# A three-block transformer on one NeuronCore: two gate products before the recurrence half, one weight split put off, squares folded inside the output units

## The chip, the core and the metric

The kernel runs on one core of a Trainium2 chip. Five engines work side by side: TensorE (matmuls), VectorE, ScalarE, GpSimd (idle here) and SyncE, which issues the DMAs. They meet only at semaphores. The metric is the device time in microseconds of one execution.

## What is computed

The input is a sequence of 256 tokens with 1024 features, in fp32. Two blocks of a first kind are followed by one of a second kind. The change lies in the first kind, between its mixer and its feed-forward:

```
merged = sigmoid(ga) * (y_attn @ w_proj_attn[l]) + sigmoid(gb) * (y_hgrn @ w_proj_hgrn[l])
x = x + merged @ w_out[l]
h = rmsnorm(x, norm_ffn[l])
g, u = split(h @ w_ffn_in[l], 2)
x = x + (silu(g) * u) @ w_ffn_out[l]
```

`y_attn` comes from a sparse attention, `y_hgrn` from a chunked gated recurrence, both 512 wide. The block of the second kind (forgetting attention, a convolution of 31 taps, another feed-forward) is not touched.

## The kernel before

**Units.** All weights are read once, in units of at most 128 x 2048 values, in a fixed order (`plan_units`). Per block of the first kind there are projections, then 4 *merge* units (256 of the 1024 outputs each, an attention half with `w_proj_attn` and an hgrn half with `w_proj_hgrn`), 4 *output* units (`w_out`), and the feed-forward: gate 0, up 0, gate 1, up 1, down 0, gate 2 and so on. I number merges and outputs 0 to 3.

**Each weight is split in two.** A matmul of this kernel is done as three, high times high, high times low and low times high (`three`, lines 507 to 509). So every unit passes ScalarE, which rounds it to `w_hi` (line 928 through the helper `f`), and VectorE, which makes `w_lo = raw - w_hi` (line 1370, `split`). There are 6 slots for raw weights and 3 (`SPL`) for split ones. `split_ahead` splits the unit three ahead of the one in hand, so a high part can start when the unit three before it is done, and SyncE refills a raw slot when its `w_lo` is written. Activations are split in the same way (`h_hi`/`h_lo`, `ya`, `yh`, `x_gained`).

**The merges.** On TensorE `first_merges` runs the attention halves of merges 0 and 1, waits for the recurrence's `yh_lo`, and runs their hgrn halves; merges 2 and 3 follow whole. Each half goes to a PSUM bank of its own. On VectorE, in `mixer`, a merge unit is: product A (`mix_a` = attention bank times `gate_a`, line 1793), product B (`mix_b` = hgrn bank times `gate_b`, line 1795), their sum (line 1797), then, behind ScalarE's `h_hi`, the low part `h_lo` (line 1799), and a `split_ahead`. `mix_a` has two buffers, `mix_b` one.

**The outputs.** TensorE's output unit 0 takes its inputs pair by pair as the `h_lo` of merges 0 to 3 are marked (`g_lo`). On VectorE an output unit is: addition into `xT` (line 1806), low part of the gained pair (`x_gained_lo`, line 1423, behind ScalarE's `x_gained_hi`), and a `split_ahead`. ScalarE does the high part, the split, and the square of the pair into `h_norm`. Gate unit 0 takes the gained pairs in turn. After output 3 VectorE folds the squares of each pair into one (`squares_folded`, line 1401), and TensorE sums them over the partitions in `norm_sum` (line 629), between gate 0 and up 0.

The order on each engine is the order in which the code is written; nothing reorders it.

Of the kernel before, what the change touches and what calls it, by code (L numbers as in the profile page):

```python
# [21 lines left out]
ALU = mybir.AluOpType  # L22
# [25 lines left out]
SPL = 3  # L48
# [61 lines left out]
UOUT = {b: min(n for n, u in enumerate(UNITS) if u[:2] == ("out", b)) for b in range(3)}  # L110
# [75 lines left out]
def build(nc, a, out):  # L186
    base = (nc.sbuf_base + 31) // 32 * 32

    def at(name, shape, dt, off_kb):
        return nc.alloc_sbuf_tensor_at(name, shape, dt, offset=base + int(off_kb * 1024))[:]  # L190
# [43 lines left out]
    mixa = [at(f"mix_a{i}", [P, 512], F32, 163 + 2 * i) for i in range(2)]  # L234
# [3 lines left out]
    ga = at("gate_a", [P, KC, T], F32, 183)  # L238
# [108 lines left out]
    def lo_at(m):  # L347

        return split_lo, m + 1
# [35 lines left out]
            ("keys_set", 1), ("decayed", 16),  # L385
            ("pair_products", 18), ("recurrence_out", 2), ("o_squares", 2), ("o_sum", 2), ("o_rstd", 2),
            ("yh_set", 1), ("yh_hi_set", 1), ("yh_lo_set", 1), ("pairs_taken", 10), ("blocks_copied", 6)))
    r_diag = Event("diagonals_taken", 2)
    g_sig = Event("gates_set", 2)
    g_mix, g_hi, g_lo = Event("mixed", 4), Event("mixed_hi", 4), Event("mixed_lo", 4)  # L390

# [23 lines left out]
    def bank(m, i=0):  # L415
        return S[BANKS[m][0][i]]
# [85 lines left out]
    def _(pe):  # L502
        cur = [0]

        def three(dst, w_h, w_l, x_h, x_l, start, stop):

            pe.matmul(dst, w_h, x_h, start=start, stop=False, skip_group_check=True)  # L507
            pe.matmul(dst, w_h, x_l, start=False, stop=False, skip_group_check=True)  # L508
            return pe.matmul(dst, w_l, x_h, start=False, stop=stop, skip_group_check=True)  # L509

        def merge_half(m, half):

            hi = wh[m % SPL].rearrange("p (k n) -> p k n", k=KC)
            lo = wl[m % SPL].rearrange("p (k n) -> p k n", k=KC)
            x_h, x_l = (yh_h, yh_l) if half else (ya_h, ya_l)
            for n in range(2):
                for k in range(4):
                    ws = (slice(None), 4 * half + k, slice(P * n, P * n + P))
                    mm = three(bank(m, half)[:, T * n:T * n + T], hi[ws], lo[ws], x_h[:, k, :], x_l[:, k, :], k == 0, k == 3)
            return mm  # L520

        def first_merges(b):

            m = cur[0]
            cur[0] += 2
            pe.wait_ge(*a_lo.upto(b))
            for i in range(2):
                pe.wait_ge(*lo_at(m + i))
                for e, c in BANKS[m + i][1]:
                    pe.wait_ge(evac[e], c)  # L530
                merge_half(m + i, 0)
            pe.wait_ge(*r_lo.at(b))
            for i in range(2):
                merge_half(m + i, 1).then_inc(unit_done, 1)
# [383 lines left out]
    def _(act):  # L918
        lane = Lane("act_lane")
        cur = [0]  # L920
# [6 lines left out]
        def f(out_, in_, func, **kw):  # L927
            return act.activation(out_, in_, func, **kw)  # L928

        def split(m):  # L930
            if m >= len(UNITS):
                return
            act.wait_ge(landed[m % RAW], LANDED[m])
            if m >= SPL:
                act.wait_ge(unit_done, m - SPL + 1)
            n = held(m)
            f(wh[m % SPL][:, 0:n], raw[m % RAW][:, 0:n], ACT.Copy).then_inc(split_hi, 1)
# [4 lines left out]
        def split_ahead():  # L942

            split(cur[0] - 1 + SPL)

        def tick(n=1):

            for _ in range(n):
                step()
                split_ahead()  # L950
# [42 lines left out]
        def square(ni, j):  # L993
            f(hn[:, 2 * j:2 * j + 2, :], xT[:, 2 * j:2 * j + 2, :], ACT.Square).then_inc(*lane.mark(n_sq))
# [53 lines left out]
        def feed_forward(b):  # L1048
            if b < 2:
                f(ones_r, ones, ACT.Copy).then_inc(*lane.mark(ones_rounded))  # L1050
            if b == 2:
                rstd(rs, A[0][:, 0:T], D, n_ms.at(5), n_rs, load=False)
                normed_hi(5)
            for i in range(FS):
                tick()
                if shifted(UNITS[here()]):
                    shifted_in(sg[i].rearrange("p (c t) -> p c t", c=2), here(), ACT.Silu, g_silu)
                elif scaled_after(UNITS[here()]):
                    if i == 0:
                        rstd(rs, A[0][:, 0:T], D, n_ms.at(2 * b + 1), n_rs)  # L1060
                    act.wait_ge(*evacuated(here()))
                    f(sg[i % 2], sg[i % 2], ACT.Silu).then_inc(*lane.mark(sg_silu))
                    if i == 0:
                        normed_hi(2 * b + 1)
                else:
                    unit_in()
                    if i >= 2:
                        act.wait_ge(*f_gu.at(b, i - 2))
                    f(sg[i % 2], bank(here()), ACT.Silu).then_inc(*emptied())
                tick()  # L1070
                act.wait_ge(*f_gu.at(b, i))
                if i >= 2:
                    act.wait_ge(unit_done, UFF[b] + 3 * (i - 2) + 5)
                f(gu_h[i % 2].rearrange("p c t -> p (c t)"), gu, ACT.Copy).then_inc(f_hi.sem, 1)
                lane.last = f_hi.at(b, i)
                if b < 2 and i - 1 in ADA_STEPS:
                    for j in ADA_GROUPS[ADA_STEPS.index(i - 1)]:
                        n = ADA_LAYER * b + j + 1
                        act.wait_ge(ada_summed, n)
                        if n > 4:  # L1080
                            act.wait_ge(ada_done, n - 4)
                        f(ada_h[:, j % 4, :], ada_sum[:, j % 4, :], ACT.Copy).then_inc(ada_hi, 1)
                if i:
                    tick()
            step()
# [8 lines left out]
        def mixer(b, x_ready):  # L1094
# [158 lines left out]
            for j in range(4):  # L1253
                step()
                act.wait_ge(*evacuated(UOUT[b] + j))
                gained_hi(2 * b + 1, lambda k: pc("norm_ffn", 8 * b + k), j)
                split_ahead()
                square(2 * b + 1, j)
            feed_forward(b)

        def qk_rstd(b, i):
# [96 lines left out]
    def _(dve):  # L1358
        lane = Lane("dve_lane")
        cur = [0]  # L1360
        tt, ts_, stt = dve.tensor_tensor, dve.tensor_scalar, dve.scalar_tensor_tensor

        def split(m):
            if m >= len(UNITS):
                return
            dve.wait_ge(split_hi, m + 1)
            if m >= SPL:
                dve.wait_ge(unit_done, m - SPL + 1)
            n = held(m)
            tt(wl[m % SPL][:, 0:n], raw[m % RAW][:, 0:n], wh[m % SPL][:, 0:n].bitcast(F32), ALU.subtract)\  # L1370
                .then_inc(split_lo, 1)
            lane.last = lo_at(m)
# [1 line left out]
        def step():  # L1374
            cur[0] += 1

        def split_ahead():

            split(cur[0] - 1 + SPL)

        def tick(n=1):

# [4 lines left out]
        def here():  # L1387
            return cur[0] - 1
# [37 lines left out]
        def squares_folded(ni, pairs=range(4)):  # L1426
            for j in pairs:
                fold(j, n_sq.at(ni, j), n_fold)
# [251 lines left out]
        def mixer(b):  # L1680
# [71 lines left out]
            for g in range(2):  # L1752
                gs = slice(2 * g, 2 * g + 2)
# [30 lines left out]
            tt(yh_l, scr, yh_h.bitcast(F32), ALU.subtract).then_inc(*lane.mark(r_lo))  # L1784
            tick()
            dve.wait_ge(*g_sig.upto(b))
            for j in range(4):
                step()
                unit_in()
                gs = slice(2 * j, 2 * j + 2)  # L1790
                if j >= 2:
                    dve.wait_ge(*g_lo.at(b, j - 2))
                tt(mixa[j % 2], bank(here(), 0), ga[:, gs, :].rearrange("p c t -> p (c t)"), ALU.mult).then_inc(*lane.step())
                dve.wait_ge(*lane.last)
                tt(mixb, bank(here(), 1), gb[:, gs, :].rearrange("p c t -> p (c t)"), ALU.mult).then_inc(*emptied())
                dve.wait_ge(*lane.last)
                tt(mixa[j % 2], mixa[j % 2], mixb, ALU.add).then_inc(*lane.mark(g_mix))
                dve.wait_ge(*g_hi.at(b, j))
                tt(hl[:, gs, :].rearrange("p c t -> p (c t)"), mixa[j % 2],
                          hh[:, gs, :].rearrange("p c t -> p (c t)").bitcast(F32), ALU.subtract).then_inc(*lane.mark(g_lo))  # L1800
                split_ahead()
            for j in range(4):
                step()
                unit_in()
                x = xT[:, 2 * j:2 * j + 2, :].rearrange("p c t -> p (c t)")
                tt(x, bank(here()), x, ALU.add).then_inc(*emptied())
                gained_lo(2 * b + 1, lambda k: pc("norm_ffn", 8 * b + k), j)
                split_ahead()
            squares_folded(2 * b + 1)
            feed_forward(b)  # L1810
            if b:
                shift_lo(0)
# [129 lines left out]
        m = here()  # L1942
# [128 lines left out]
```

## Time and profile before

| | us |
|---|---|
| median of 3 runs | 1211.08 (1210.41 to 1212.88) |
| profiled execution, its own time | 1210.74 |
| its span, first to last instruction | 1209.0 |
| TensorE busy in the span | 1152.7 |
| VectorE / ScalarE busy | 862.9 / 622.2 |
| mean granted TensorE clock | 0.992 |

A timeline row has the start in us from the span's start, the duration in us, engine, line of the kernel, operation, output and inputs, shape and count. In brackets stands how long the engine had been idle before, and the instruction that released it. Consecutive matmuls overlap: the distance between two starts is what one costs. A row of the waiting list has the engine and line that waited, for whom, the total, how often, and the longest. A row of the windows has the stretch, its length, the busy time of TensorE with its count, the granted clock (1.00 is full speed), and the share and rate of the DMA engines. The stretch of interest is 200 to 252 us in block 0, and 621 to 674 us in block 1.

### The profile page before, as it was taken

The page shows a single profiled execution, that of the slowest core. Times are in us where ns is not written, and L with a number is a line of the kernel's source. Part 1 is how long each engine was busy: PE and PEld are TensorE (multiplying, and loading weights), DVE is VectorE, ACT ScalarE, POOL GpSimd, SP SyncE. Part 2 cuts the span into 40 slices and gives each one's busy share as a digit, 9 for nine tenths or more (in the row PEclk, how much of TensorE's full clock was granted, in tenths as well). Part 3 has the DMA queues.
Part 4 walks back from the last instruction along what each step waited for, and adds up shares of the span by engine and source line. Part 5 has one row for each costly group of instructions (what it writes and reads, how often), then busy time and mean ns, then how long its engine had stood idle before and what let it go on. Part 6 is the DMA issues. An engine that isn't in the chain of part 4 may idle for free.

```text
span 1209.0 us, 21217 instructions
## 1 busy us (share of the span) xinstructions
PE 1152.7 (95%) x8966; PEld 1115.6 (92%) x8966; DVE 862.9 (71%) x1404; ACT 622.2 (51%) x762; POOL 0.2 (0%) x4
## 2 busy tenths in 40 slices
PE   6999999999999999999999999999999989999996
PEld 5789899999999998998999999999988889999996
DVE  6996474777888779955757778887799757544543
ACT  7676336454434466753464544344587455443333
POOL 0000000000000000000000000000000000000000
PEclk9999999999999999999999999999999999999998
DMA  9555433656879555463336568795544332655511
GB/s 348 157 163 175 140 106 105 227 192 210 280 255 322 171 177 162 142 187 126 111 112 216 191 211 281 253 320 180 165 140 140 99 111 75 207 188 193 176 36 35
DMA packets 177615, 214.16 MB, mean 177 GB/s; under 512 B 3696, under 2 KB 160752, under 8 KB 177520
## 3 DMA queue, kind: packets, MB, share of 16 engines
q1 hardware_dynamic: 176800, 211.86, 53.4%
q8 instruction: 71, 1.16, 0.4%
q10 hardware_dynamic: 720, 0.94, 0.2%
q14 instruction: 24, 0.20, 0.0%
HBM read 211.74 MB, written 1.05 MB: 176 GB/s over the span
## 4 chain that ended last, share of the span: by engine, by line
PE 71%; DVE 19%; ACT 6%; issue 2%; DMA 1%; SPq 0%; DVEq 0%; ACTq 0%
PE stream L507 16%; PE stream L508 15%; PE stream L509 15%; DVE w_lo L1370 7%; PE steps L507 5%; PE steps L509 5%; PE steps L508 5%; PE steps L844 2%; ACT w_hi L928 2%; DVE conv_acc L1926 2%; PE steps L697 1%; PE stream L718 1%; DMA raw<-in_w_in 1%; ACT probs L928 1%; DVE h_norm L1450 1%
## 5 line engine op out<-in xcount | busy, mean ns | idle before, releaser
L1370 DVE TENSOR_TENSOR w_lo<-raw,w_hi 128x2048 fp32r<-128x2048 f32 (+2 forms) x178 | 401.4, 2266 | 205.3 <-ACT w_hi L928 203.7
L928 ACT ACTIVATE w_hi<-raw 128x2048 fp32r<-128x2048 f32 (+2 forms) x178 | 336.5, 1894 | 326.1 <-PE stream L509 294.2
L507 PE MATMUL stream<-h_hi,w_hi 128*128 128x256 f32 x1576 | 450.6, 286 | 12.1 <-DVE w_lo L1370 7.4
L509 PE MATMUL stream<-h_hi,w_lo 128*128 128x256 f32 x1576 | 446.5, 283 | 0.0
L508 PE MATMUL stream<-h_lo,w_hi 128*128 128x256 f32 x1576 | 446.5, 283 | 0.0
L507 PEld LDWEIGHTS stream<-h_hi,w_hi 128*128 128x128 f32 x1576 | 303.0, 192 | 16.3 <-DVE w_lo L1370 10.3
L508 PEld LDWEIGHTS stream<-h_lo,w_hi 128*128 128x128 f32 x1576 | 303.1, 192 | 0.5 <-issue 0.5
L509 PEld LDWEIGHTS stream<-h_hi,w_lo 128*128 128x128 f32 x1576 | 303.0, 192 | 0.0
L507 PE MATMUL steps<-gu_hi,w_hi 128*128 128x256 f32 x528 | 149.8, 284 | 1.4 <-DVE gu_lo L1665 1.4
L508 PE MATMUL steps<-gu_lo,w_hi 128*128 128x256 f32 x528 | 149.4, 283 | 0.0
L509 PE MATMUL steps<-gu_hi,w_lo 128*128 128x256 f32 x528 | 149.4, 283 | 0.0
L507 PEld LDWEIGHTS steps<-gu_hi,w_hi 128*128 128x128 f32 x528 | 101.3, 192 | 1.8 <-issue 1.8
L508 PEld LDWEIGHTS steps<-gu_lo,w_hi 128*128 128x128 f32 x528 | 101.3, 192 | 0.0
L509 PEld LDWEIGHTS steps<-gu_hi,w_lo 128*128 128x128 f32 x528 | 101.3, 192 | 0.0
L1619 DVE SCALAR_TENSOR_TENSOR ada_sum<-ada_raw,c_act,ada_sum 128x256 f32<-128x256 f32 x168 | 81.5, 485 | 6.0
L928 ACT ACTIVATE gu_hi<-gu 128x512 fp32r<-128x512 f32 x33 | 20.9, 633 | 102.6 <-DVE gu L1661 98.5
L580 PE MATMUL stream<-w_hi,x_gained_hi 128*128 128x512 f32 (+1 forms) x96 | 37.3, 388 | 11.3 <-DVE w_lo L1370 11.3
L1926 DVE SCALAR_TENSOR_TENSOR conv_acc<-conv_in,params,conv_acc 128x256 f32<-128x256 f32 x90 | 38.9, 488 | 1.0
L1665 DVE TENSOR_TENSOR gu_lo<-gu,gu_hi 128x512 fp32r<-128x512 f32 x33 | 22.9, 692 | 23.1 <-ACT gu_hi L928 23.1
L507 PE MATMUL stream<-x_gained_hi,w_hi 128*128 128x256 f32 x128 | 36.6, 286 | 0.0
L508 PE MATMUL stream<-x_gained_lo,w_hi 128*128 128x256 f32 x128 | 36.2, 283 | 0.0
L509 PE MATMUL stream<-x_gained_hi,w_lo 128*128 128x256 f32 x128 | 36.2, 283 | 0.0
(296 smaller groups left out, 1653.4 us busy)
## 6 DMA issues: line engine op xcount, KB each, us to landing
raw<-in_w_ffn_in SPq DMA_DIRECT2D x66, 1024.0 KB, 5.3
raw<-in_w_in SPq DMA_DIRECT2D x54, 1024.0 KB, 5.4
raw<-in_w_ffn_out SPq DMA_DIRECT2D x33, 1024.0 KB, 5.2
ada_raw<-in_ada_w SPq DMA_DIRECT2D x24, 1024.0 KB, 6.4
raw<-in_w_out SPq DMA_DIRECT2D x8, 1024.0 KB, 5.1
raw<-in_w_proj_attn SPq DMA_DIRECT2D x8, 512.0 KB, 3.5
raw<-in_w_proj_hgrn SPq DMA_DIRECT2D x8, 512.0 KB, 4.5
raw<-in_w_o SPq DMA_DIRECT2D x4, 1024.0 KB, 4.9
```

The costliest lines, as they stand in the source:

```text
L507: pe.matmul(dst, w_h, x_h, start=start, stop=False, skip_group_check=True)
L508: pe.matmul(dst, w_h, x_l, start=False, stop=False, skip_group_check=True)
L509: return pe.matmul(dst, w_l, x_h, start=False, stop=stop, skip_group_check=True)
L580: pe.matmul(dst, h_h[:, k0 + k, ts], hi[:, k, :], start=k0 + k == 0, stop=False)
L697: mm = pe.matmul(pv[:, DH * h:DH * h + DH], prT[:, h, s, :], v[:, s, DH * h:DH * h + DH], start=s == 0, stop=s == qt)
L718: mm = pe.matmul(conv_bank[:, 0:T], diag[j], upad[:, 3, j:j + T], start=j == 0, stop=j == CONV_K - 1)
L844: mm = pe.matmul(pair_bank(i, g)[:, c - 2 * g, t, :], hk[:, c, P * t:P * t + P], qp[:, c, P * tq:P * tq + P], start=True, stop=True)
L928: return act.activation(out_, in_, func, **kw)
L1370: tt(wl[m % SPL][:, 0:n], raw[m % RAW][:, 0:n], wh[m % SPL][:, 0:n].bitcast(F32), ALU.subtract)\
L1619: ins = stt(acc, w[:, k, :], cact[:, k:k + 1], acc, ALU.mult, ALU.add)
L1665: tt(gu_l[i % 2].rearrange("p c t -> p (c t)"), gu, gu_h[i % 2].rearrange("p c t -> p (c t)").bitcast(F32), ALU.subtract).then_inc(*lane.m ...
L1926: ins = stt(cv[:, c, :], src, w, cv[:, c, :], ALU.mult, ALU.add)
```

## The change

On TensorE the last matmul of the attention halves of merges 0 and 1 now steps a new semaphore, `merge_half`. On VectorE products A of merges 0 and 1 are issued together, when these halves are done and the gates are set, before the wait for merge 0; products A of merges 2 and 3 stay in their units. The `split_ahead` at the end of merge 2 (it makes the low part of output unit 1) is left out there and done behind the work of merge 3, ahead of that unit's own. In the output units the squares of pair j-1 are folded at the end of unit j, for j = 1 and 2, and those of pairs 2 and 3 in unit 3 ahead of its `split_ahead`, on both VectorE and (for the square) ScalarE.

```
@@ first_merges
-                merge_half(m + i, 0)
+                merge_half(m + i, 0).then_inc(m_half.sem, 1)
@@ ScalarE, output units
-                split_ahead()
+                if j < 3:
+                    split_ahead()
                 square(2 * b + 1, j)
+            split_ahead()
             feed_forward(b)
@@ VectorE, split_ahead
-        def split_ahead():
-
-            split(cur[0] - 1 + SPL)
+        def split_ahead(behind=(0,)):
+
+            for n in behind:
+                split(cur[0] - 1 + SPL - n)
@@ VectorE, merges
             dve.wait_ge(*g_sig.upto(b))
+
+            def gate_a(j):
+                tt(mixa[j % 2], bank(UOUT[b] - 4 + j, 0), ga[:, 2 * j:2 * j + 2, :].rearrange("p c t -> p (c t)"), ALU.mult)\
+                    .then_inc(*lane.step())
+
+            for j in range(2):
+                dve.wait_ge(*m_half.at(b, j))
+                gate_a(j)
             for j in range(4):
                 step()
                 unit_in()
                 gs = slice(2 * j, 2 * j + 2)
                 if j >= 2:
                     dve.wait_ge(*g_lo.at(b, j - 2))
-                tt(mixa[j % 2], bank(here(), 0), ga[:, gs, :].rearrange("p c t -> p (c t)"), ALU.mult).then_inc(*lane.step())
+                    gate_a(j)
...
-                split_ahead()
+                if j != 2:
+                    split_ahead(range(j // 3, -1, -1))
@@ VectorE, output units
                 gained_lo(2 * b + 1, lambda k: pc("norm_ffn", 8 * b + k), j)
-                split_ahead()
-            squares_folded(2 * b + 1)
+                if j < 3:
+                    split_ahead()
+                squares_folded(2 * b + 1, range(j - 1, j + j // 3) if j else ())
+            split_ahead()
             feed_forward(b)
```

On VectorE, at the start of the merges of block 0, stood before (`w_lo_60` is the low part of merge 2, `w_lo_58` that of merge 3; `mix_a_104` and `mix_a_105` are the two buffers):

```order
L1784 TENSOR_TENSOR yh_lo<-scratch,yh_hi 128x1024
L1370 TENSOR_TENSOR w_lo_60<-raw_51,w_hi_57 128x2048
L1793 TENSOR_TENSOR mix_a_104<-stream,gate_a 128x512
L1795 TENSOR_TENSOR mix_b<-stream,gate_b 128x512
L1797 TENSOR_TENSOR mix_a_104<-mix_a_104,mix_b 128x512
L1799 TENSOR_TENSOR h_lo<-mix_a_104,h_hi 128x512
L1370 TENSOR_TENSOR w_lo_58<-raw_52,w_hi_55 128x2048
L1793 TENSOR_TENSOR mix_a_105<-stream,gate_a 128x512
```

and stands now:

```order
L1787 TENSOR_TENSOR yh_lo<-scratch,yh_hi 128x1024
L1372 TENSOR_TENSOR w_lo_60<-raw_51,w_hi_57 128x2048
L1792 TENSOR_TENSOR mix_a_104<-stream,gate_a 128x512
L1792 TENSOR_TENSOR mix_a_105<-stream,gate_a 128x512
L1806 TENSOR_TENSOR mix_b<-stream,gate_b 128x512
L1808 TENSOR_TENSOR mix_a_104<-mix_a_104,mix_b 128x512
L1810 TENSOR_TENSOR h_lo<-mix_a_104,h_hi 128x512
L1372 TENSOR_TENSOR w_lo_58<-raw_52,w_hi_55 128x2048
```

Product A of merge 1 has moved from behind the split of merge 3 to directly behind product A of merge 0.

On VectorE, from the end of merge 2 through merge 3 to output unit 0 (`w_lo_60` is here the low part of output 1, `w_lo_58` that of output 2), stood before:

```order
L1799 TENSOR_TENSOR h_lo<-mix_a_104,h_hi 128x512
L1370 TENSOR_TENSOR w_lo_60<-raw_54,w_hi_57 128x2048
L1793 TENSOR_TENSOR mix_a_105<-stream,gate_a 128x512
L1795 TENSOR_TENSOR mix_b<-stream,gate_b 128x512
L1797 TENSOR_TENSOR mix_a_105<-mix_a_105,mix_b 128x512
L1799 TENSOR_TENSOR h_lo<-mix_a_105,h_hi 128x512
L1370 TENSOR_TENSOR w_lo_58<-raw_49,w_hi_55 128x2048
L1806 TENSOR_TENSOR xT<-stream,xT 128x512
```

and stands now:

```order
L1810 TENSOR_TENSOR h_lo<-mix_a_104,h_hi 128x512
L1792 TENSOR_TENSOR mix_a_105<-stream,gate_a 128x512
L1806 TENSOR_TENSOR mix_b<-stream,gate_b 128x512
L1808 TENSOR_TENSOR mix_a_105<-mix_a_105,mix_b 128x512
L1810 TENSOR_TENSOR h_lo<-mix_a_105,h_hi 128x512
L1372 TENSOR_TENSOR w_lo_60<-raw_54,w_hi_57 128x2048
L1372 TENSOR_TENSOR w_lo_58<-raw_49,w_hi_55 128x2048
L1818 TENSOR_TENSOR xT<-stream,xT 128x512
```

The low part of output 1 stands behind the fourth `h_lo` instead of ahead of the fourth product A.

On VectorE, from output unit 2 to the feed-forward (`w_lo_58` is the low part of up 0, `w_lo_59` that of gate 1, `w_lo_60` that of up 1), stood before:

```order
L1806 TENSOR_TENSOR xT<-stream,xT 128x512
L1423 SCALAR_TENSOR_TENSOR x_gained_lo<-xT,params,x_gained_hi 128x256 x2
L1370 TENSOR_TENSOR w_lo_58<-raw_52,w_hi_55 128x2048
L1806 TENSOR_TENSOR xT<-stream,xT 128x512
L1423 SCALAR_TENSOR_TENSOR x_gained_lo<-xT,params,x_gained_hi 128x256 x2
L1370 TENSOR_TENSOR w_lo_59<-raw_53,w_hi_56 128x2048
L1401 TENSOR_TENSOR h_norm<-h_norm 128x256 x4
L1370 TENSOR_TENSOR w_lo_60<-raw_54,w_hi_57 128x2048
```

and stands now:

```order
L1818 TENSOR_TENSOR xT<-stream,xT 128x512
L1426 SCALAR_TENSOR_TENSOR x_gained_lo<-xT,params,x_gained_hi 128x256 x2
L1372 TENSOR_TENSOR w_lo_58<-raw_52,w_hi_55 128x2048
L1404 TENSOR_TENSOR h_norm<-h_norm 128x256
L1818 TENSOR_TENSOR xT<-stream,xT 128x512
L1426 SCALAR_TENSOR_TENSOR x_gained_lo<-xT,params,x_gained_hi 128x256 x2
L1404 TENSOR_TENSOR h_norm<-h_norm 128x256 x2
L1372 TENSOR_TENSOR w_lo_59<-raw_53,w_hi_56 128x2048
L1372 TENSOR_TENSOR w_lo_60<-raw_54,w_hi_57 128x2048
```

Of the four folds (`h_norm<-h_norm`) one now stands ahead of the addition of output 3, one ahead of that of output 2, and two ahead of the split of gate 1.

## Rows read from the trace of the kernel before

**Rows 1.** The page, busy time, share of the span and instructions of each engine:

```profile
PE 1152.7 (95%) x8966; PEld 1115.6 (92%) x8966; DVE 862.9 (71%) x1404; ACT 622.2 (51%) x762; POOL 0.2 (0%) x4
```

**Rows 2.** What TensorE waited for, whole span: total, times, longest:

```profile
PE stream L507 <- DVE h_lo L1799: 3.8, 2, 1.9
```

**Rows 3.** Timeline of TensorE, block 0: attention half, merge 3 and output 0, sum of squares:

```profile
195.86 0.28 PE L507 MATMUL stream<-ya_hi,w_hi 128*128 128x256 f32 x1
...
218.77 0.28 PE L509 MATMUL stream<-yh_hi,w_lo 128*128 128x256 f32 x1
218.89 0.28 PE L507 MATMUL stream<-h_hi,w_hi 128*128 128x256 f32 x1
...
223.09 0.28 PE L509 MATMUL stream<-h_hi,w_lo 128*128 128x256 f32 x1
225.29 0.38 PE L507 MATMUL stream<-h_hi,w_hi 128*128 128x256 f32 x1 [1.92 <-DVE h_lo L1799]
...
250.54 1.99 PE L629 MATMUL steps<-h_norm,ones 128*128 128x256 f32 x8 [0.52 <-DVE h_norm L1401]
```

**Rows 4.** Timeline of TensorE, block 1, same places:

```profile
646.94 0.38 PE L507 MATMUL stream<-h_hi,w_hi 128*128 128x256 f32 x1 [1.92 <-DVE h_lo L1799]
...
673.60 1.99 PE L629 MATMUL steps<-h_norm,ones 128*128 128x256 f32 x8 [0.44 <-DVE h_norm L1401]
```

**Rows 5.** Windows of TensorE behind the two stops, clock in the fourth column:

```profile
226.00:229.00 3.00, 3.00 (x28) 1.00 0.90 281
...
648.10:651.50 3.40, 3.40 (x18) 0.50 1.02 336
651.50:655.00 3.50, 3.50 (x32) 1.00 0.69 267
```

**Rows 6.** Timeline of VectorE, block 0, merge 0 and the end of merge 3:

```profile
200.64 2.28 DVE L1370 TENSOR_TENSOR w_lo<-raw,w_hi 128x2048 fp32r<-128x2048 f32 x1
204.76 0.69 DVE L1793 TENSOR_TENSOR mix_a<-stream,gate_a 128x512 f32<-128x512 f32 x1 [1.84 <-PE stream L509]
205.49 0.69 DVE L1795 TENSOR_TENSOR mix_b<-stream,gate_b 128x512 f32<-128x512 f32 x1
...
208.21 2.29 DVE L1370 TENSOR_TENSOR w_lo<-raw,w_hi 128x2048 fp32r<-128x2048 f32 x1
...
224.55 0.69 DVE L1799 TENSOR_TENSOR h_lo<-mix_a,h_hi 128x512 fp32r<-128x512 f32 x1 [0.70 <-ACT h_hi L928]
225.16 2.29 DVE L1370 TENSOR_TENSOR w_lo<-raw,w_hi 128x2048 fp32r<-128x2048 f32 x1
```

**Rows 7.** Timeline of VectorE, block 0, output units 0 and 1 and the folds:

```profile
227.36 0.69 DVE L1806 TENSOR_TENSOR xT<-stream,xT 128x512 f32<-128x512 f32 x1
229.02 0.88 DVE L1423 SCALAR_TENSOR_TENSOR x_gained_lo<-xT,params,x_gained_hi 128x256 fp32r<-128x256 f32 x2 [0.98 <-ACT x_gained_hi L928]
...
233.04 0.68 DVE L1806 TENSOR_TENSOR xT<-stream,xT 128x512 f32<-128x512 f32 x1
...
250.07 1.42 DVE L1401 TENSOR_TENSOR h_norm<-h_norm 128x256 f32<-128x256 f32 x4
```

**Rows 8.** Timeline of ScalarE, block 0, gates, two weight parts, the last square:

```profile
200.78 1.92 ACT L928 ACTIVATE gate_b<-gate_b 128x2048 f32<-128x2048 f32 x1
204.75 1.92 ACT L928 ACTIVATE w_hi<-raw 128x2048 fp32r<-128x2048 f32 x1 [2.05 <-PE stream L509]
...
219.15 1.92 ACT L928 ACTIVATE w_hi<-raw 128x2048 fp32r<-128x2048 f32 x1 [0.29 <-PE stream L509]
...
247.73 0.61 ACT L928 ACTIVATE h_norm<-xT 128x512 f32<-128x512 f32 x1
```

**Rows 9.** Timeline of SyncE's DMA queue, block 0:

```profile
202.95 19.23 SPq L476 DMA_DIRECT2D raw<-in_w_ffn_in  x4
225.33 0.37 SPq L455 DMA_DIRECT2D ada_raw<-in_ada_w  x1
```

**Rows 10.** The page, DMA issues: count, KB of each, median us to landing:

```profile
raw<-in_w_ffn_in SPq DMA_DIRECT2D x66, 1024.0 KB, 5.3
```

More of the change, by code:

```diff
@@ L387, in build @@
             ("yh_set", 1), ("yh_hi_set", 1), ("yh_lo_set", 1), ("pairs_taken", 10), ("blocks_copied", 6)))
-    r_diag = Event("diagonals_taken", 2)
+    r_diag, m_half = Event("diagonals_taken", 2), Event("merge_half", 2)
     g_sig = Event("gates_set", 2)
```

## Prediction

> **What bounds the kernel now.** Read the busy times first: TensorE is busy for 1152.7 of 1209.0 us [rows 1], so only two things shorten this kernel: less idle time of TensorE, or a fuller clock. Next comes the view of what TensorE waits for. One of its rows is for `h_lo` of line 1799, 3.8 us in two pieces of 1.9 [rows 2], one in each of the two first blocks. Then the timeline shows the place. Output unit 0 starts at 218.89, takes its inputs pair by pair, and stops after 36 of its 48 matmuls, at 223.09; the next one starts at 225.29 [rows 3]. What it lacks is the low part of the fourth merged pair, which VectorE writes from 224.55 on [rows 6]. The normal distance between matmuls is 0.12 us (192 of them from 195.86 to 218.89 [rows 3]), so a unit of 48 takes 5.76 us and the stop costs 2.20 - 0.12 = 2.08 us. At the end of the same stretch the sum of squares (line 629) waits another 0.52 us for the folded squares, and starts at 250.54 [rows 3]. The second block has the same rows 421.65 us later, with a stop that ends at 646.94 and the sum of squares at 673.60 [rows 4].
>
> From stop to sum of squares block 0 takes 250.54 - 225.29 = 25.25 us, block 1 takes 673.60 - 646.94 = 26.66. The windows explain the difference: behind the first stop the granted clock stays 1.00, while behind the second it is 0.50 from 648.1 to 651.5 (1.2 instead of 2.4 GHz) and then 1.00 again [rows 5]. So this profiled run paid 26.66 - 25.25 = 1.41 us for a dip that came 1.2 us after TensorE had stood still for 2.08.
>
> VectorE is what TensorE waits for here. Per merge unit it does product A, product B, their sum, the low part (behind ScalarE's high part), and one weight low part `w_lo`. From A to the start of the next `w_lo` it is 208.21 - 204.76 = 3.45 us, and `w_lo` takes its place for 227.36 - 225.16 = 2.20 [rows 6, 7]: 5.65 us in all. Merges 0 to 3 keep it busy without a gap from 204.76 to 227.36, while TensorE, which does the hgrn halves of merges 0 and 1 in 2.88 us each, is through with merge 3 at 218.89.
>
> **The change, part by part, in block 0.** I follow VectorE through the new order, always with the old rows' distances.
>
> *Products A of merges 0 and 1 early.* They need the attention halves (done by 201.61, 48 matmuls after 195.86), and still wait for the gates: `gate_b` is ready at 200.78 + 1.92 = 202.70 [rows 8], the `w_lo` ahead ends at 200.64 + 2.28 = 202.92 [rows 6]. Two products of 0.69 then end by 204.3, in the 1.84 us in which VectorE was idle until 204.76 [rows 6]. They cost nothing; without that cover they would cost up to 1.4. Product B of merge 0 now starts at 204.76. That saves 0.73 (204.76 to 205.49 [rows 6]), but ScalarE is on `w_hi` until 204.75 + 1.92 = 206.67 [rows 8], and the high part comes behind it, so only 0.37 is left: the next `w_lo` starts at 207.84 instead of 208.21. Merge 1 is 5.65 - 0.73 = 4.92 us: 212.76. Merge 2: product A at 212.76 + 2.20 = 214.96, end of its work at 218.41.
>
> *Low part of output unit 1 put off.* VectorE would now be free at 218.41, but merge 3 is released only at 219.15 (ScalarE's `w_hi`, held by the same unit, starts then [rows 8]). So product A starts at 219.15, and the low part of pair 3 ends 3.45 + 0.08 later (225.24 against 225.16 [rows 6]), at 222.68. TensorE wants it at 223.09 + 0.12 = 223.21. The stop of 2.08 us is gone, with 0.5 us to spare. What is late next is the weight part that was put off: `w_lo` of output 1 runs from 222.60 to 224.88, and TensorE wants it at 218.89 + 5.76 = 224.65. I take a new stop of 0.3 us there (bounds 0.2 to 0.6), output 1 starting at 224.95. `w_lo` of output 2 follows to 227.08, and has until 230.7.
>
> *Its DMA.* The slot that this low part frees was refilled at the end of SyncE's row, 202.95 + 19.23 = 222.18 [rows 9]; it becomes 224.9. Queued behind it are one modulation load, which waited until 225.33 anyway [rows 9], and one down-projection load. The refilled slot is read at 249 at the earliest, so 24 us cover a transfer whose median to landing is 5.3 us [rows 10]. I put it at nothing.
>
> *Squares folded inside the output units.* An addition into `xT` starts at 227.00, 0.36 earlier than the 227.36 of before. A VectorE round there was 233.04 - 227.36 = 5.68 us [rows 7], 0.08 under TensorE's. One fold is 1.42 / 4 = 0.36 [rows 7]. Rounds 1 and 2 carry one each, so the fourth addition starts at 227.00 + 17.04 + 0.72 = 244.76, and the low part of its gained pair ends 1.66 + 0.88 later [rows 7], at 247.30. TensorE reaches gate unit 0 at 224.95 + 0.1 for the restart + 17.28 = 242.33 and wants that pair 4.32 later, at 246.65. So part of the gain is given back: a second new stop of 0.7 us. The folds are the price (0.72), and their return is that the sum of squares no longer waits: folds 2 and 3 end near 248.0, before the last 12 matmuls of gate 0 do. These run from 247.35, and the sum of squares starts at 247.35 + 0.1 + 1.44 + 0.16 = 249.05. Against 250.54 that is **1.49 us**.
>
> ScalarE's square of pair 3 ahead of the last `w_hi` is what lets fold 3 go at 247.6; behind it, it was over only at 247.73 + 0.61 = 248.34 [rows 8]. The `w_hi` goes back by 0.6, and its `w_lo` ends near 251.0 with the next unit due at 256.6. From there on TensorE waits for nothing until the end of the feed-forward, so the lead of 1.49 carries through.
>
> The new semaphore step at the end of each attention half: the last matmul of merge 3, which has such a step, is at 218.77 and the next at 218.89, the usual 0.12 [rows 3], so four more cost nothing. The Trainium skill (TensorE: Matmul & The Clock Gate, section The cost: per-tile semaphore tail) counts about 26 ns for each increment; by that, as an estimate, four would be 0.1 us and the forecast 1206.8. The trace does not agree.
>
> **Sum.** Block 0: 1.49. Block 1, same rows 421.65 later: sum of squares at 646.94 + (249.05 - 225.29) = 670.70 instead of 673.60, so 2.90, of which 1.41 is the clock, if TensorE, with 0.3 and 0.7 us stops in place of 2.08, keeps it. Together 4.39: 1210.74 (this execution; its span is 1209.0) becomes 1206.35. The median of before is 1211.08, 0.34 above the profiled run: **1206.7 us**.
>
> **Rivals.**
>
> *The clock dip is luck.* Two equal stops were followed by one dip, so a run may have none, one or two, and the median of before need not hold the one I count; or it comes again after the new stops. Then only 2 x 1.49 = 2.98 is left: 1208.1. For it: block 0 kept its clock after the same stop. Against it: the dip that there is follows a stop. The Trainium skill (TensorE: Matmul & The Clock Gate, section The HAM clock gate) takes idle TensorE as the cause of a halved clock and says that its moment varies between runs of one kernel; the two blocks agree with the second half of that.
>
> *The stop only moves.* In merge 3 the high part must not be behind `w_hi` of output 2, which ends at 219.15 + 1.92 = 221.07 against the 221.33 at which it is wanted: 0.26 to spare. If this or the put-off `w_lo` comes a microsecond later than in my walk, output 1 waits 1.3 instead of 0.3, VectorE is late by as much in the output rounds, and a block gains about 0.5: 1210.1 without the clock, within the noise.
>
> *The folds hold VectorE up (slower).* Fold j-1 waits for ScalarE's square, which stands behind a `w_hi` of 1.9 us. If each of the two folds ahead of additions 2 and 3 waited that long, gate unit 0 would stop 3.8 us longer per block: 1206.7 + 7.6 = 1214.3. It turns slower than before from a wait of 1.1 us per fold (4 x 1.1 = 4.4). Against it: each fold stands a round of 5.7 us behind the square of its pair, and ScalarE is through with the last square at 248.34, 1.7 us before the first fold starts now [rows 7, 8], so it is not the late one there.
>
> **How the numbers follow.** Forecast 0.52, the dip as luck 0.27, the moved stop 0.14, the folds 0.05, 0.02 for what I don't see. For the range I take the forecast with its bounds (0.2 to 0.6 at output 1, a restart of 0.1 more or less at each stop, 0.7 us between medians of three): from 1205.6. Up it takes in the second case with the same spread: 1209.0. What can be told from no change is about 0.2%, 2.4 us, thus 1208.66: all of the forecast and most of the second case lie below, 0.79 with the rest; the moved stop and the tail of the second make 0.16; the folds 0.05.
>
> **What would show it.** In the changed trace: two products A back to back before 204.7; no wait for `h_lo` of pair 3; instead one of some 0.3 us for `w_lo` at output 1 and one of some 0.7 for `x_gained_lo` at gate unit 0; the sum of squares at 249.05 (670.7 in block 1) with no wait of its own; a granted clock of 1.00 in both stretches. I am wrong if the `h_lo` wait is still there, if either new wait is above 1.5 us, or if the clock is 0.50 somewhere between 205 and 260 or 627 and 680.

## The result, and the profile after

| | before | after |
|---|---|---|
| median, us | 1211.51 (4 runs, 1210.41 to 1212.88) | 1204.97 (4 runs, 1204.12 to 1205.77) |
| ratio, 95% interval | | 0.9949 (0.9937 to 0.9961) |
| profiled execution, its own time | 1210.74 | 1204.12 |
| its span | 1209.0 | 1202.3 |
| mean granted clock in it | 0.992 | 0.996 |

The changed kernel is 6.5 us faster, 4.4 had been forecast (the median of before was 1211.08 then), and the range, whose lower end was 1205.6, does not hold 1204.97.

The page's busy times come first. TensorE's is 3.8 us smaller than in [rows 1], with the same number of matmuls: matmuls at half clock last longer, so a part of the gain looks like clock; the windows further down show where.

```profile
PE 1148.9 (96%) x8966; PEld 1112.0 (92%) x8966; DVE 862.7 (72%) x1404; ACT 621.2 (52%) x762; POOL 0.2 (0%) x4
```

The timeline of TensorE in block 0, the places of [rows 3]. This execution stands 0.18 us later than the old one at 196.04 (195.86 there), so distances from that row are to be compared:

```profile
196.04 0.28 PE L507 MATMUL stream<-ya_hi,w_hi 128*128 128x256 f32 x1
...
224.72 0.28 PE L509 MATMUL stream<-h_hi,w_lo 128*128 128x256 f32 x1
225.07 0.39 PE L507 MATMUL stream<-h_hi,w_hi 128*128 128x256 f32 x1
...
246.65 0.28 PE L509 MATMUL stream<-x_gained_hi,w_lo 128*128 128x256 f32 x1
247.42 0.39 PE L507 MATMUL stream<-x_gained_hi,w_hi 128*128 128x256 f32 x1 [0.49 <-DVE x_gained_lo L1426]
...
248.84 0.28 PE L509 MATMUL stream<-x_gained_hi,w_lo 128*128 128x256 f32 x1
248.95 0.81 PE L629 MATMUL steps<-h_norm,ones 128*128 128x256 f32 x3
```

Output 0 runs through: the wait for `h_lo` is gone. Output 1 starts 0.35 behind its predecessor's last matmul instead of 0.12, a stop of 0.23 (0.3 forecast). Gate unit 0 stops for 0.77 - 0.12 = 0.65 us before its fourth pair (0.7 forecast), and the sum of squares follows the last matmul of gate 0 by 0.11 without a wait. Block 1 shows the same. From here on I use one measure, **D**: the distance from the first matmul of merge 0's attention half to the first matmul of the sum of squares. Before it is 250.54 - 195.86 = 54.68 us in block 0 [rows 3], and after it is 248.95 - 196.04 = 52.91; 52.92 in block 1.

VectorE in the same stretch, to set against [rows 6] and [rows 7]:

```profile
200.82 2.29 DVE L1372 TENSOR_TENSOR w_lo<-raw,w_hi 128x2048 fp32r<-128x2048 f32 x1
203.02 1.28 DVE L1792 TENSOR_TENSOR mix_a<-stream,gate_a 128x512 f32<-128x512 f32 x2
204.88 0.69 DVE L1806 TENSOR_TENSOR mix_b<-stream,gate_b 128x512 f32<-128x512 f32 x1 [0.57 <-PE stream L509]
...
207.40 0.69 DVE L1810 TENSOR_TENSOR h_lo<-mix_a,h_hi 128x512 fp32r<-128x512 f32 x1 [1.11 <-ACT h_hi L928]
...
219.28 0.69 DVE L1792 TENSOR_TENSOR mix_a<-stream,gate_a 128x512 f32<-128x512 f32 x1 [0.42 <-PE stream L509]
...
222.12 0.69 DVE L1810 TENSOR_TENSOR h_lo<-mix_a,h_hi 128x512 fp32r<-128x512 f32 x1 [0.70 <-ACT h_hi L928]
222.73 4.49 DVE L1372 TENSOR_TENSOR w_lo<-raw,w_hi 128x2048 fp32r<-128x2048 f32 x2
227.13 0.68 DVE L1818 TENSOR_TENSOR xT<-stream,xT 128x512 f32<-128x512 f32 x1
...
244.82 0.68 DVE L1818 TENSOR_TENSOR xT<-stream,xT 128x512 f32<-128x512 f32 x1
246.48 0.88 DVE L1426 SCALAR_TENSOR_TENSOR x_gained_lo<-xT,params,x_gained_hi 128x256 fp32r<-128x256 f32 x2 [0.98 <-ACT x_gained_hi L928]
247.28 0.75 DVE L1404 TENSOR_TENSOR h_norm<-h_norm 128x256 f32<-128x256 f32 x2
```

The two products A are over at 204.3, under TensorE's hgrn half of merge 0. In merge 3 VectorE now waits for TensorE (0.42), where in the old kernel TensorE waited for VectorE's low part. The two weight parts that follow merge 3 stand one behind the other, and the fourth addition starts at 244.82 - 0.18 = 244.64 on the old clock, against 244.76 in the prediction's walk.

The windows show the full clock where the old kernel had 1.00 in one block and 0.50 in the other [rows 5]:

```profile
226.00:229.00 3.00, 3.00 (x27) 1.00 0.98 303
...
646.00:650.00 4.00, 4.00 (x36) 1.00 1.06 361
```

The clock differs in a third place, which the change does not touch. In the third block TensorE stands still for 5.6 us, and the clock goes to one half towards the end of it. These are windows of the kernel before, then of the changed one:

```profile
996.30:999.70 3.40, 2.20 (x10) 0.50 0.00 0
999.70:1003.00 3.30, 3.30 (x14) 0.50 0.00 0
...
991.70:995.00 3.30, 2.79 (x13) 0.50 0.00 0
995.10:998.40 3.30, 3.30 (x23) 1.00 0.00 0
```

Set against each other matmul by matmul, the two profiled executions part at these places:

| where | us gained |
|---|---|
| block 0, merges to the first low-part matmul of up 0 (252.49 - 195.86 = 56.63 before, 250.80 - 196.04 = 54.76 after) | 1.87 |
| one matmul of the recurrence in block 1 | 0.40 |
| block 1, the same stretch as in block 0 | 3.29 |
| third block, half clock for 3.4 us instead of 6.8 | 1.28 |
| start of the kernel | -0.18 |

These make the 6.6 us between 1210.74 and 1204.12.

### The profile page after: what moved, and what is told of

Read it like the earlier page. It is cut to its first block, busy times and chain, and to the rows that moved or that the text cites. A ratio compares the mean times of both kernels' runs of the same rounds, so it can differ in the third digit from the quotient of the medians.

```text
span 1202.3 us, 21221 instructions
## 1 busy us (share of the span) xinstructions
PE 1148.9 (96%) x8966; PEld 1112.0 (92%) x8966; DVE 862.7 (72%) x1404; ACT 621.2 (52%) x762; POOL 0.2 (0%) x4
## 3 DMA queue, kind: packets, MB, share of 16 engines
q8 instruction: 71, 1.16, 0.4%
## 4 chain that ended last, share of the span: by engine, by line
PE 71%; DVE 18%; ACT 7%; issue 2%; DMA 1%; SPq 0%; DVEq 0%; ACTq 0%
PE stream L507 16%; PE stream L509 15%; PE stream L508 15%; DVE w_lo L1372 7%; PE steps L507 5%; PE steps L509 5%; PE steps L508 5%; ACT w_hi L928 3%; PE steps L844 2%; DVE conv_acc L1940 2%; PE steps L697 1%; PE stream L718 1%; DMA raw<-in_w_in 1%; ACT probs L928 1%; DVE h_norm L1453 1%
```

## Experiments

The kernels of one group ran on the same chip beside runs of the kernel before. Each diff is against the changed kernel.

### One part taken back at a time

**e1, products A back in their units.**

```
-            for j in range(2):
-                dve.wait_ge(*m_half.at(b, j))
-                gate_a(j)
             for j in range(4):
...
-                    gate_a(j)
+                gate_a(j)
```

> The changed kernel, with the products A of merges 0 and 1 back in their units. D is the distance from the first matmul of the attention half of merge 0 to the first matmul of the sum of squares; it is 54.68 us before and 52.91 after in block 0. By the walk of the prediction product A costs VectorE 0.73 once more, of which 0.37 was hidden by ScalarE's high part, so all that follows is 0.36 later: no stop for h_lo (0.15 us spare), a stop of 0.6 at output 1, one of 0.65 at gate unit 0, D = 53.3 in both blocks, 0.7 us slower in all than the changed kernel. Rival, the early products carry the gain: the stop for h_lo comes back with over 1 us, D = 54 or more.

Measured: D = 53.32 in both blocks, stops of 0.63 at output 1 and 0.66 at gate unit 0, none for `h_lo`; 1205.98 us, ratio to before 0.9955 (0.9938 to 0.9971). In D the early products are worth 0.4 us a block, not more. Two waits of VectorE hide the rest of what they save: the one for `h_hi` in merge 0 (1.11 instead of 0.70 in e1) and the one for TensorE in merge 3 (0.42). They also take away the 0.40 of the recurrence in block 1, as told below.

**e2, low part of output 1 back in merge 2.**

```
-                if j != 2:
-                    split_ahead(range(j // 3, -1, -1))
+                split_ahead()
```

> The changed kernel, with the low part of output unit 1 back in merge 2. By the walk the fourth h_lo is ready at 224.1 (before's clockwork), so output 0 stops for 0.9 us, output 1 and gate unit 0 not at all, and the sum of squares starts at the same place within 0.2 us: D = 53.0, time as the changed kernel's within 0.4 us. Rival, the put-off part is what removes the stop and is worth it: D is 0.9 or more longer (53.8), 1.8 us slower in all.

Measured: D = 53.08, 1205.47 us, ratio 0.9952 (0.9937 to 0.9966). The wait for `h_lo` is back, shorter than before:

```profile
224.56 0.39 PE L507 MATMUL stream<-h_hi,w_hi 128*128 128x256 f32 x1 [0.99 <-DVE h_lo L1810]
```

It is 1.16 us (I had 0.9), and it costs only 0.17 in D, because with it go the two stops of the changed kernel, 0.23 at output 1 and 0.65 at gate unit 0: VectorE's first addition starts 30.57 us behind merge 0 instead of 31.09, TensorE arrives later, and it waits neither at gate unit 0 nor at the sum of squares.

**e3, folds and last square back at the end.**

```
-                if j < 3:
-                    split_ahead()
-                squares_folded(2 * b + 1, range(j - 1, j + j // 3) if j else ())
-            split_ahead()
+                split_ahead()
+            squares_folded(2 * b + 1)
```

(and on ScalarE the last `split_ahead` ahead of the last `square`)

> The changed kernel, with the four folds back behind the last split of the output units and ScalarE's last square behind its last weight part. By the walk gate unit 0 doesn't stop, but VectorE reaches the folds only at 249.7, so the sum of squares waits some 2 us: D = 54.3, 1.4 us more per block than the changed kernel, 2.8 in all. Rival, the removed stop is the gain whatever the folds do: D = 52.3 (the changed kernel less its stop of 0.65 at gate unit 0).

Measured: D = 54.26 and 54.27; 1209.62 us (10 runs), ratio 0.9987 (0.9977 to 0.9996). The wait for `h_lo` is gone here too, and nearly all of its time has come up again at the sum of squares:

```profile
249.88 0.72 PE L629 MATMUL steps<-h_norm,ones 128*128 128x256 f32 x1 [1.87 <-DVE h_norm L1402]
```

That is a stop of 2.03 us, and in both blocks the clock fell right behind it (windows of TensorE in e3):

```profile
250.00:253.40 3.40, 3.40 (x9) 0.50 0.83 258
673.20:676.60 3.40, 3.40 (x13) 0.51 0.91 296
```

### One part alone

**e4, folds alone** (the edits of e1 and e2 together).

> Only the folds are moved: products A and the low part of output 1 stand as before. By the walk the stop of 2.08 us for h_lo stays, gate unit 0 doesn't stop, the sum of squares doesn't wait: D = 54.0, 0.7 us less per block than before. If the dip of the clock follows the stop of 2.08 us, a dip shows in at least one of the two blocks here as in the kernel before, and the time is 1.4 us or more above what D says (1211.5 - 1.4 = 1210.1 with before's dips). Rival, dips fall anywhere: the clock rows of e1, e2 and e3, which have no such stop, show as many between 205 and 260 or 625 and 680.

Measured: D = 54.00 in block 0 and 55.50 in block 1, where the clock fell 1.0 us after the end of the stop of 2.07; 1209.14 us (10 runs), ratio 0.9986 (0.9976 to 0.9995). The forecast time of 1210.1 was 1 us too high; 0.7 of that is its base, 1211.5, where the kernel before had a median of 1210.76 beside e4. Traces of kernels without a stop of 2 us (e1, e2) show no dip in these stretches.

**e9, early products alone** (the edits of e2 and e3 together).

> Only the products A of merges 0 and 1 are moved. The stop for h_lo shrinks to that of e2 (1.16 us), and the additions into xT run 1.1 us ahead of before until they meet TensorE's end of output 3, after which the folds stand behind the last split as before: D = 53.8, 0.9 us less per block than before, and no dip of the clock. Rival, the sum of squares is held by the folds wherever the stop is: D = 54.3 or more.

Measured: D = 53.74 and 53.75, a stop of 1.15 for `h_lo` and one of 0.66 at the sum, no dip in either block; 1207.03 us, ratio 0.9961 (0.9946 to 0.9976).

**e10, put-off part alone** (the edits of e1 and e3 together).

> Only the low part of output 1 is put off. No stop for h_lo, one of 0.63 us at output 1 as in e1; VectorE's additions start where they did before, and the folds stand at the end: D = 54.6, as before's 54.7 although the stop of 2.08 is gone; the sum of squares waits for the folds by over 1.5 us instead, and if that wait reaches 2 us a dip can follow it as in e3. Rival, the removed stop shows in the time: D = 53.2.

Measured: D = 54.67 in both blocks, within 0.01 that of the kernel before without a dip; 1210.83 us (10 runs), ratio 0.9997 (0.9987 to 1.0006). The stop of 2.08 is replaced by these two:

```profile
225.78 0.39 PE L507 MATMUL stream<-h_hi,w_hi 128*128 128x256 f32 x1 [0.48 <-DVE w_lo L1370]
...
251.02 0.48 PE L629 MATMUL steps<-h_norm,ones 128*128 128x256 f32 x1 [1.85 <-DVE h_norm L1402]
```

In block 1 a dip followed the second of these stops, and none did in block 0.

Alone, the early products, the put-off part and the folds save 0.94, 0.01 and 0.68 us of D, 1.63 together; with each other 1.77. None of them alone brings the 2.08 us of the list of waits: with the folds last, the sum of squares waits for them, and with the folds moved alone the stop stays. Two of them can even be worse than one: early products with the put-off part (e3) have D = 54.26, early products alone (e9) 53.74. In e3 VectorE waits 0.42 for TensorE in merge 3 with the put-off weight part still ahead of it, so the first addition starts 31.09 us behind merge 0 instead of 30.57, and the folds at the end are later by these 0.52.

### The stop that the change brought in

**e5, all folds in output unit 3.** The new stop at gate unit 0 is the price of the two folds ahead of additions 2 and 3. Behind the fourth `x_gained_lo` there is room for all four.

```
-                squares_folded(2 * b + 1, range(j - 1, j + j // 3) if j else ())
+                squares_folded(2 * b + 1, range(4 if j == 3 else 0))
```

> The changed kernel, with all four folds in output unit 3, between its x_gained_lo and its split, instead of one each at the end of units 1 and 2. By the walk the fourth x_gained_lo comes 0.72 us earlier, which ends the stop of 0.65 at gate unit 0, and the four folds (1.42 us) still end 0.1 us before the last matmul of gate 0. D goes from 52.91 to 52.2 in both blocks, the time from the changed kernel's by -1.4 us. Rival, the stop moves to the sum of squares, which waits for the folds: D stays at 52.7 or more.

**e6, the changed kernel again**, beside it.

> The changed kernel once more, as the measure for e5 and for the clock. D = 52.9 in both blocks, no dip of the clock between 190 and 260 or 610 and 680, median 1205.0.

Measured: e5 D = 52.25 and 52.24, 1203.67 us (5 runs, 1202.49 to 1204.69), ratio to before 0.9938 (0.9925 to 0.9950); e6 D = 52.93 and 52.92, 1204.63 us (5 runs, 1203.98 to 1205.28), ratio 0.9947 (0.9934 to 0.9959). D is 0.68 less per block, as expected; the medians differ by 1.0 us, where 1.4 was expected, within the spread of the runs. VectorE and TensorE in e5:

```profile
245.40 0.88 DVE L1426 SCALAR_TENSOR_TENSOR x_gained_lo<-xT,params,x_gained_hi 128x256 fp32r<-128x256 f32 x2 [0.98 <-ACT x_gained_hi L928]
246.20 1.43 DVE L1404 TENSOR_TENSOR h_norm<-h_norm 128x256 f32<-128x256 f32 x4
247.73 2.29 DVE L1372 TENSOR_TENSOR w_lo<-raw,w_hi 128x2048 fp32r<-128x2048 f32 x1
```

```profile
247.75 0.28 PE L509 MATMUL stream<-x_gained_hi,w_lo 128*128 128x256 f32 x1
247.86 0.60 PE L629 MATMUL steps<-h_norm,ones 128*128 128x256 f32 x2
```

The folds end at 247.63 and the sum starts at 247.86, with no bracket. By D and by the median this is the fastest kernel of the study; the intervals of its ratio and of e6's overlap.

**e11, e5 with the low part of output 1 back in merge 2.**

> As e5 (products A early, folds in output unit 3), with the low part of output 1 back in merge 2. TensorE stops 1.16 us for h_lo as in e2 and nowhere else: D = 53.1, 0.85 more than e5, so that the put-off part is worth five times what it is in e2 against the changed kernel (0.16). Rival, its worth is the same 0.16 with any place of the folds: D = 52.4.

Measured: D = 53.09 in both blocks; 1204.75 us, ratio 0.9943 (0.9928 to 0.9958). So the put-off part is worth 0.84 us a block once VectorE is not the bound at gate unit 0, 0.17 in the change as it was made, and nothing by itself (e10).

### The clock

**e7, e8 and e12, the kernel before again**, for more traces of its two stops.

> The kernel before once more. D = 54.7 in a block without a dip, 56.1 in one with. If each stop of 2.08 us is followed by a dip with a chance well over one half, the mean granted clock over all its runs is 0.003 below the changed kernel's (two dips of 3.4 us at half clock are 3.4 us of lost clock). If dips fall anywhere, the two kernels have the same mean clock.

> The kernel before for a third trace: two more stops of 2.08 us, to count how many are followed by a dip. Dips from the stops: at least one of the two. Dips anywhere: none, since the other kernels' traces show none in these stretches without a stop of 2 us.

> The kernel before for a fourth trace, to count dips behind its two stops of 2.08 us: with four dips behind six stops so far, one or two are expected; none would bring it to four of eight.

Measured: e7 1211.12 us (11 runs; ratio 1.0001, 0.9992 to 1.0010), D = 56.09 and 56.08, a dip behind both stops; e8 D = 54.66 and 56.09 in 1210.49 us; e12 54.67 and 56.09 in 1210.48. The windows of e7:

```profile
226.20:229.60 3.40, 3.40 (x19) 0.50 0.98 321
649.40:652.80 3.40, 3.40 (x18) 0.51 1.05 352
```

Counted over all traces of the study, in the stretch from the merges to up 0 of both blocks:

| stop in the stretch | stretches | with a dip |
|---|---|---|
| 2.07 or 2.08 us, for `h_lo` (before four times, e4) | 10 | 6 |
| 2.01 to 2.03 us, for the folds (e3, e10) | 4 | 3 |
| at most 1.16 us (after, e1, e2, e5, e6, e9, e11) | 14 | 0 |

A dip costs 56.09 - 54.67 = 1.42 us of D in the kernel before, and 55.50 - 54.00 = 1.50 in e4, where the sum of squares has no wait that hides a part of it. In block 0 it followed 2 of 7 long stops, in block 1 all 7; why the blocks differ is open.

The length of the stop is not the whole condition. The third block has shorter stops of its own, the same in all 14 traces. Behind one in which TensorE was idle for 1.39 us a dip of 3.4 us came in 4 of them (e12, e1, e2, e9), 1.2 to 1.9 us after its end. Behind one of 1.79 us, 45 us later, none came in any. The first, and the dip behind it, in e12 (a timeline row, then a window):

```profile
921.54 2.02 PE L677 MATMUL steps<-k_and_cum,q_and_pick 72*128 72x128 f32 x16 [1.39 <-ACT k_and_cum L928]
...
923.50:926.80 3.30, 3.30 (x18) 0.50 0.35 94
```

What sets the two apart was not tried.

The mean granted clock over many runs points the same way, but can't be turned into a number of dips. It is 0.9916 over 47 runs of the kernel before and 0.9942 over 9 of the changed one. The difference of 0.0027 is 3.2 us of clock lost less, with about 1.1 either way by the scatter of the runs, and one dip of 3.4 us at one half loses 1.7. But the mean covers the whole span, and behind TensorE's last matmul, which ends at 1192.2 in the changed kernel, the clock goes to one half as well:

```profile
1196.50:1202.30 5.80, 0.00 (x0) 0.50 0.41 139
```

That end lasts 5.9 us here, 9.2 in e6 and 7.7 to 8.8 in the four traces of before, and costs no time of TensorE. And the dip behind the 5.6 us stop of the third block lasts 6.8 us in nine traces (the four of before, e2, e4, e5, e9, e10) and 3.4 in five (after, e6, e1, e3, e11). Its length does not go with the long stops in blocks 0 and 1: e2, e5 and e9 have none and show 6.8, e3 has them and shows 3.4.

The times say how many dips the kernel before has behind its two stops. The traces with one ran 1210.48, 1210.49 and 1210.74 us, the one with two 1211.99. The 47 runs beside the experiments have a median of 1210.90, and 15 of them lie at 1211.4 or above. So, as an estimate from the times alone, most runs have one dip and about one in three has two.

## Why the prediction was right and wrong

**The place and the mechanism: right.** TensorE's wait for VectorE's fourth `h_lo` was the loss, and it is gone. VectorE wasn't quite without a gap there: it waits 0.70 us for ScalarE in each merge unit, as in [rows 6]. The walk's 5.65 us per unit include that wait.

**The early products at no cost, worth 0.36: right for D.** e1 measures 0.41.

**The put-off part leaves a stop of 0.3 at output 1: right,** 0.23; its DMA cost nothing, as said.

**The folds bring a stop of 0.7 at gate unit 0 and take the wait off the sum: right,** 0.65 and 0. The prediction didn't ask whether the same folds could stand behind the fourth pair, where they cost nothing (e5).

**The sum of squares at 249.05, 1.49 us per block: the size was off.** Measured 1.87. From the first matmul of gate 0's fourth pair to the sum I counted 0.1 + 1.44 + 0.16 = 1.70, and it is 248.95 - 247.42 = 1.53: the 0.16 isn't there. The walk ran 0.11 late by then (247.35 against 247.42 - 0.18). And I forgot that the old kernel pays a restart at the sum too: its first matmul is 0.1 us longer behind a wait. Both blocks together 0.77 us.

**Nothing outside the two stretches: the step that failed.** The sum has a term for each block and none for the rest, with no reason beyond TensorE's waiting for nothing up to the end of the feed-forward. In the profiled executions 4.39 was forecast and 6.62 measured. Of the 2.23 between, 0.77 is the size above, 0.01 the dip in block 1, 1.28 the half clock in the third block and 0.40 the recurrence in block 1, less 0.18 at the start (2.28; the 0.05 more is rounding). At one matmul there the kernel before waits 0.40 us for VectorE (line 1602), the changed one doesn't:

```profile
597.53 0.49 PE L844 MATMUL steps<-hgrn_q_decayed,hgrn_k 128*128 128x128 f32 x2 [0.40 <-DVE hgrn_k L1602]
```

That wait is in all 7 traces of kernels without the early products (before four times, e1, e4, e10), and in none of the 7 with them, though the work there is the same. Without them VectorE starts 0.37 us later behind the same release. What the two more waits in VectorE's program have to do with it was not tried.

In the medians the two terms that D and the traces fix, 0.77 and 0.40, take the forecast of 1206.7 to 1205.5, already below the range's end of 1205.6. Measured were 1204.97, and 1204.63 in e6. The 0.6 to 0.9 left is about half a dip. A shorter dip in the third block or a second one behind the stops of before can make it, and which of them does, and how often, is open.

**The dip of the clock behind the two stops: right in the profiled executions, its frequency not known.** One dip was counted at 1.41 and one was there, of 1.42. That the profiled execution was near the median in this was luck: its kernel has a dip behind 5 of its 8 traced stops. The rival then went only one way: none or one dip in the median of before, so less gain. With two the same sum gives 1206.7 - 1.4 = 1205.3, which the range leaves out too.

**The rivals.** The moved stop did not come true for the change; it is what e3 and e10 show. The folds that hold VectorE up did not either: one fold alone between a `w_lo` and an addition costs 0.34 (238.47 to 238.81 in the changed kernel), as counted. The estimate of 0.1 us for four more semaphore steps isn't seen: from merge 0's first matmul to merge 2's, with the two steps of a block between them, it is 207.37 - 195.86 = 11.51 before and 207.56 - 196.04 = 11.52 after, where the estimate would give 0.05 more.

## What to carry to other kernels

A stop is worth what stands behind it allows: follow the engine that was late past the stop to the next place where the two meet, and see which arrives last there. Here taking away a stop of 2.08 us brought nothing (e10) until the folds behind it were moved too, and one of the three parts is worth nothing alone. Before a dip of the clock goes into a sum, take its frequency from several executions, and look at every dip of the trace, also those far from the change: here the largest term that was missing lay in a block that the change doesn't touch. One trace shows only that a dip can happen, and a mean clock over the whole span also counts stretches in which TensorE has nothing to do.

## What the runs showed of the hardware

- In the stretches of the change, stops of TensorE of 2.0 to 2.1 us were followed by 3.4 us at half clock in 9 of 14 cases, whatever was waited for; the 14 stretches without such a stop had no dip. In the third block a dip came behind 1.39 us of idle TensorE in 4 of 14 traces, and behind 1.79 us in none. A dip cost 1.42 us, 1.50 in e4.
- The first matmul behind a wait is 0.38 or 0.39 us long instead of 0.28, and the next starts 0.22 instead of 0.12 us behind it: about 0.1 us for each stop, seen for stops from 0.23 to 2.08 us.
- On VectorE two products A of 128x512 in fp32, the second of which doesn't wait for the first, took 1.28 us together, a distance of 1.28 - 0.69 = 0.59; product A to product B, which waits for product A, is 0.73 [rows 6]. Such a wait costs about 0.14 us even where nothing is late.
